# A constant table cut from 696 to 680 columns, so that every tile behind it starts 64 bytes earlier

## The reference, cut to what matters

```python
def moe_swiglu(h, w_router, w_gate, w_up, w_down):
    logits = jnp.einsum('bsd,de->bse', h, w_router)
    top_val, top_idx = lax.top_k(logits, TOP_K)
    top_w = jax.nn.softmax(top_val, axis=-1)
    gates = jnp.sum(jax.nn.one_hot(top_idx, N_EXPERTS) * top_w[..., None], axis=-2)
    for e in range(N_EXPERTS):
        out = out + gates[..., e:e + 1] * swiglu(h, w_gate[e], w_up[e], w_down[e])
```

## Time and profile before

| | before |
|---|---|
| runs, median of 3 | 2091.82 us (2089.37 to 2091.98) |
| profiled execution, its own time | 2090.75 us |
| its span, first to last instruction | 2088.6 us |
| mean granted TensorE clock | 0.943 |
| TensorE matmul busy | 1956.6 us (94%) |
| VectorE, ScalarE busy | 1639.9 us, 1138.5 us |
| moved by DMA | 551.08 MB, mean 264 GB/s |

### The profile page before, as it was taken

The page is one execution under the profiler, slowest core; times in us unless marked ns, Lnnn a source line. Parts: engine busy times, 40 slices in busy tenths (PEclk is TensorE's granted clock), DMA queues, the critical chain, the costliest instruction groups (busy, mean ns, idle before and its releaser), DMA issues.

```text
span 2088.6 us, 29232 instructions
## 1 busy us (share of the span) xinstructions
PE 1956.6 (94%) x9196; PEld 1613.7 (77%) x9196; DVE 1639.9 (79%) x2173; ACT 1138.5 (55%) x1616; POOL 36.1 (2%) x47
## 2 busy tenths in 40 slices
PE   2999999989899999999999999988899999789998
PEld 1987888867688888888888888766778888677886
DVE  6988886757798888888888989896676669666554
ACT  1434444443677767776776777654444444545443
POOL 2000000000000000000000000000000000000000
PEclk9999999977899999999999999987699999779999
DMA  8867996545599999999999999947368875735662
GB/s 297 328 242 265 342 357 196 146 153 180 188 359 333 359 329 368 328 365 327 349 346 341 354 338 354 346 159 215 120 211 267 272 234 151 238 116 177 213 217 74
DMA packets 368361, 551.08 MB, mean 264 GB/s; under 512 B 35715, under 2 KB 292998, under 8 KB 368230
## 3 DMA queue, kind: packets, MB, share of 16 engines
q1 hardware_dynamic: 365280, 547.81, 77.3%
q10 hardware_dynamic: 2118, 1.46, 0.2%
q0 software_dynamic: 832, 0.30, 0.1%
HBM read 548.39 MB, written 1.08 MB: 263 GB/s over the span
## 4 chain that ended last, share of the span: by engine, by line
PE 83%; DVE 10%; ACT 3%; issue 3%; DMA 1%; POOL 0%; DVEq 0%; ACTq 0%; POOLq 0%
PE ps L401 23%; PE ps L403 23%; PE ps L402 23%; PE ps L877 3%; PE ps L866 2%; DVE units_low L396 2%; PE ps L1046 2%; PE ps L931 2%; DVE mod_acc L1546 1%; PE ps L728 1%; PE ps L854 1%; DVE x_tokens L1573 1%; ACT prob L1239 1%; DVE x_normed L1572 1%; DMA mod_in<-in_mod_w 1%
## 5 line engine op out<-in xcount | busy, mean ns | idle before, releaser
L396 DVE TENSOR_TENSOR units_low<-raw_units,units_high 128x1024 fp32r<-128x1024 f32 (+2 forms) x840 | 983.0, 1220 | 121.9 <-ACT units_high L392 115.7
L392 ACT ACTIVATE units_high<-raw_units 128x1024 fp32r<-128x1024 f32 (+2 forms) x840 | 845.0, 1058 | 244.3 <-PE ps L403 232.8
L401 PE MATMUL ps<-units_high,hT_high 128*128 128x512 f32 (+2 forms) x1576 | 624.1, 396 | 4.3 <-DVE act L1642 2.9
L402 PE MATMUL ps<-units_low,hT_high 128*128 128x512 f32 (+2 forms) x1576 | 621.3, 394 | 0.0
L403 PE MATMUL ps<-units_high,hT_low 128*128 128x512 f32 (+2 forms) x1576 | 621.0, 394 | 0.0
L401 PEld LDWEIGHTS ps<-units_high,hT_high 128*128 128x128 f32 (+1 forms) x1576 | 297.4, 189 | 75.8 <-DVE act L1642 3.6
L403 PEld LDWEIGHTS ps<-units_high,hT_low 128*128 128x128 f32 (+1 forms) x1576 | 297.2, 189 | 68.3
L402 PEld LDWEIGHTS ps<-units_low,hT_high 128*128 128x128 f32 (+1 forms) x1576 | 297.4, 189 | 67.5 <-issue 0.2
L401 PE MATMUL ps<-units_high,aT_high 128*128 128x512 f32 x632 | 259.6, 411 | 1.1 <-DVE qkT L1783 0.6
L403 PE MATMUL ps<-units_high,aT_low 128*128 128x512 f32 x632 | 249.1, 394 | 0.0
L402 PE MATMUL ps<-units_low,aT_high 128*128 128x512 f32 x632 | 248.8, 394 | 0.0
(11 more groups left out here) (273 smaller groups left out, 1486.9 us busy)
## 6 DMA issues: line engine op xcount, KB each, us to landing
raw_units<-in_moe_w_gate SPq DMA_DIRECT2D x352, 256.0 KB, 4.0
raw_units<-in_moe_w_up SPq DMA_DIRECT2D x352, 256.0 KB, 4.7
raw_units<-in_moe_w_down SPq DMA_DIRECT2D x176, 512.0 KB, 4.9
mod_in<-in_mod_w SPq DMA_DIRECT2D x96, 512.0 KB, 5.5
mod_in<-in_w_mod SPq DMA_DIRECT2D x96, 512.0 KB, 5.0
raw_units<-in_w_gu SPq DMA_DIRECT2D x176, 256.0 KB, 3.3
raw_units<-in_w_down SPq DMA_DIRECT2D x44, 512.0 KB, 4.2
raw_units<-in_w_in SPq DMA_DIRECT2D x32, 512.0 KB, 7.2
```

Of the source, the lines that this page charges most:

```text
L392: eng.activation(whi[:rows, n % H, 0:width], raw[:rows, n % R, 0:width], ACT.Copy).then_inc(f.hi, 1)
L396: eng.tensor_tensor(low[:rows, n % R, 0:width], raw[:rows, n % R, 0:width], whi[:rows, n % H, 0:width].bitcast(F32), ALU.subtract).then_in ...
L401: pe.matmul(dst, ah, bh, start=start, stop=False, **kw)
L402: pe.matmul(dst, ah, bl, start=False, stop=False, **kw)
```

## The change

The short ramp is left out; the stacked identity takes its eight columns at 512; the table ends at column 680. The comparison of the router reads the first eight columns of the long ramp (the same numbers, 0 to 7). The row of the table becomes 2720 bytes, and every tile behind it starts 64 bytes earlier: mod_in at 85440, raw_units at 101824 (397 times 256, and 192), units_high at 146880, qkv at 175136, masks at 214560. The four tiles ahead of the table, and the table itself, stay.

```diff
-C_ID, C_ONE, C_LT, C_IO, C_I8, C_FREQ, C_COS, C_SIN = 0, 128, 256, 384, 512, 520, 552, 616
-C_ST = 680
-C_W = 696
+C_ID, C_ONE, C_LT, C_IO, C_ST, C_FREQ, C_COS, C_SIN = 0, 128, 256, 384, 512, 520, 552, 616
+C_W = 680
...
     c[:, C_IO:C_IO + P] = np.arange(P)
-    c[:, C_I8:C_I8 + E] = np.arange(E)
     c[0:2 * E, C_ST:C_ST + E] = np.concatenate([np.eye(E), np.eye(E)])
...
-        i8 = table[:, C_I8:C_I8 + E][:, None, :].broadcast_to((P, T, E))
+        i8 = table[:, C_IO:C_IO + E][:, None, :].broadcast_to((P, T, E))
```

## The result

The changed kernel takes **2068.95 us** in the median of four runs (2066.5 to 2073.85), against 2091.9 us before (2089.37 to 2092.85). The ratio is 0.9895 with a 95% interval of 0.9872 to 0.9918: faster by 1%, where I had forecast no change. The profiled execution took 2066.5 us, its span 2064.3 us against 2088.6. In the changed file all lines behind the constants stand two lower (L401 of before is L399), and the order of instructions is the same on every engine.

What follows compares the result with a forecast made beforehand. The prediction took TensorE as the bound, with loads close behind. All terms (named instructions, table's load, the 64 bytes on each engine and on loads) were zero, summing to 0 us: 2091.8 us, range 2085.0 to 2098.0.

Steps and rivals of the forecast that it cites:

- What bounds the kernel: Expert passes of 100.10 us: TensorE sets the pace, loads close behind, queue 1 filling 99.0% of the DMA engines' time.
- the two ways that I named: Whole kernel: either TensorE instructions change in length, or packets grow so much longer that loads overtake TensorE.
- The instructions of the diff and the table's load: Router comparisons and small matmuls: zero, 1.8 us either way at most; table's load: zero, gain between 0 and 0.1 us.
- The 64 bytes on TensorE: 6624 matmuls from units at moved addresses: taken as zero, range 1 ns each, 6.6 us either way.
- the sign that I had named: Signs of a right forecast: matmul median within 1 ns of 393 ns, expert passes of 100.1 us.
- VectorE and ScalarE: Unit splits: VectorE zero, within 0.8 us over 840 splits; ScalarE shows nothing below 1 us per unit.
- Loads: Loads into raw_units and mod_in: packets between 0 and 15% longer, taken as zero.
- rival 1: Expert loop: packets grow and loads become the bound; 4% gives 2116 us, 15% gives 2204 us; chance 0.06.
- My landing row of masks: 256 KB load into masks, 96 past, lands in 2.9 us, into raw_units in 3.3 us; basis for zero on loads.
- The 19% of the page: Expert loads by the skill's page: off-multiple packets cost 1.19 times as much, 118 us a pass, 2235 us in all.
- Rival 2: Attention stages' clock back sooner, 2084.3 us, or fewer memory collisions, matmuls 1 ns shorter, 2085.2 us; chance 0.13.
- the 0.75 on no change: Whole kernel: chance 0.75 that the time stays 2091.8 us, within 2087.6 to 2096.0.

Runs made afterwards that it cites:

- e1: Changed kernel plus 64 unused bytes behind the table, so every tile behind it starts where it did before the change; 2091.18 us, 1.0001 to the kernel before.
- e2: Changed kernel plus 64 unused bytes ahead of x_tokens, units back at their bytes before the change; 2071.7 us, 0.9912 to the kernel before.
- e10: e5 plus 32 unused bytes ahead of x_tokens, all distances still 0, every tile 32 past a multiple of 64; 2057.26 us, 0.9848 to the kernel before.
- e5: Changed kernel plus 64 unused bytes behind the table and 128 behind aT_low, hT and aT at distance 0 from units; 2058.98 us, 0.9842 to the kernel before.
- e16: e5 plus 128 unused bytes ahead of x_tokens, distances still 0, raw_units at a multiple of 256; 2057.91 us, 0.9844 to the kernel before.

## Why the prediction was wrong

**What bounds the kernel** was right: TensorE sets the pace of the passes before, after and in all runs, and loads stay just behind it. Of the two ways that I named in which the time could move, it was the first.

**The instructions of the diff and the table's load**, both at zero: right. e1 has all of it and none of the bytes, 1.0001.

**The 64 bytes on TensorE** is the step that failed. I compared the median durations of a matmul from units_low and one from y_low, took 393 and 392 ns as "no dearer", and bounded the term at 1 ns either way. There are two faults in it. The first is the quantity: the duration is that of a record that overlaps with the next, 393 ns where the starts are 233 ns apart. The changed kernel lowers the median duration by 1 ns and the distance of the starts by 3.5; the sign that I had named, a median within 1 ns of 393, would even have passed, and only that of the pass length failed. The second is the comparison: I looked at where one operand lies by itself, and e2 and e10 show that this has no effect at all. What counts is how the operands lie to each other, which the units of different slots (4096 bytes apart) could not show either, since the steps are multiples of 256. The row of y_low could not have warned of it even by its starts. By the tiles' sizes y_low and its weights scatter_hot lie at distance 0, before as after, and yet, of each four such matmuls, the starts behind the first pair are mostly 229 to 236 ns apart, here 0.46 us for two steps in the kernel before:

```profile
572.75 0.39 PE L1061 MATMUL ps<-y_low,scatter_hot 128*128 128x512 f32 x1
...
573.21 0.40 PE L1061 MATMUL ps<-y_low,scatter_hot 128*128 128x512 f32 x1
```

The term measured 4728 x 3.5 = 16 us, 2.5 times the end that I gave it. That end was worked out from the grain of a record's duration, and no row bounded the distance of the starts, 232.6 ns, from below: e5 brought it to 226.8.

**VectorE and ScalarE**: right, the mean time of a unit moved by under 2 ns on both engines (VectorE 1219.8 to 1218.3 ns, ScalarE 1058.1 to 1057.8).

**Loads**: the sum was right with nothing, the reason was not. Packets did grow, as rival 1 said. In the window of the earlier trace rows the changed kernel moved 1.99 MB at 104.3%, 23.8 KB/us an engine against 24.8, which is the 4% of that rival. In the passes the 34.7 MB took 102.5% of 99.2 us where they took 99.0% of 100.1, 2.6% more. What rival 1 had wrong is the point from which that decides: passes fell to 98.21 us with the longer packets of e5, and stayed there when e16 took the growth away. A share of 99%, or of 103.9%, is thus not a limit reached. My landing row of masks spoke against a price, and was too coarse to see one. The 19% of the page was also applied to all packets, though a third of a pass's bytes (w_down) moves in packets of 4096 bytes, for which the same count gives 134 beats instead of 128, 5%; the estimate by the page should have been about 14%, still far above the 3 to 5% that the runs show.

**Rival 2** had the right sign with 0.13, and one of its mechanisms is shown: a faster matmul (6.6 us forecast, 16 found). The clock that comes back sooner (one attention stage by 4 us) is seen in the changed kernel's profile, but some executions of the kernel before have it as well, so that part of the agreement is luck. It named the memory read "at once" by several engines; the split by VectorE's and ScalarE's work shows no part of theirs above 0.4 ns.

The range ended at 2085.0 because the bound on the matmul term was too narrow, and the 0.75 on no change rested on the same rows.

## What to carry to other kernels

Where TensorE runs 32-bit products back to back, lay out all operands that follow each other there (both weights, both moving tiles) at equal addresses modulo 256 bytes; it was worth 1.6% here against the kernel before, for pads of 192 bytes (e5), and the 64 bytes of the table alone 1%. Read a pipelined matmul's price from the distance of successive starts, never from its record's duration. When a neutral change moves the time, pad the kernel back to its old places first: it is one line.

## What the runs showed of the hardware

- The pace of 512-column matmuls in long rows of three-matmul products was 226.8 ns (hT; 229.0 with aT, the median step 227 for both) with all operands at distance 0 modulo 256, 229 to 230 at 64, 232.5 at 128, 233.3 at 192 and at 32 and 96. The absolute place made no difference (e10), nor did the share of the DMA engines (e5 and e16, 103.9% and 99.1%), and the work of VectorE and ScalarE made 0.4 ns at most. Distance 0 alone is not enough: rows of four matmuls with scatter_hot, which lie at it by the tiles' sizes, took mostly 229 to 236 ns a step.
- The Trainium skill (SBUF — State Buffer, Who interferes with whom) gives TensorE two read ports, one for the moving operand and one for weights, calls them independent, and says that TensorE never waits for another engine. The runs agree with the last part. With the independence they agree only if the loss arises elsewhere than at the ports: moving one operand by 64 bytes changed the pace by up to 9 ns for a matmul, and no run here shows where that loss arises.
- Packets of loads whose destination in the on-chip memory lies off a multiple of 256 bytes took more of the DMA engines' time: 102.5% against 99.7% of a pass (changed kernel and e2, equal passes), 103.9% against 99.1% (e5 and e16, equal passes). The Trainium skill (DMA: Bandwidth & Descriptors, How a descriptor splits into AXI transactions) has a rule of that kind for the start of a descriptor; the runs agree in sign for the destination, at 3 to 5% where my estimate by the page was 19%, and is 14% with the longer packets of w_down counted by their own size.
